# One weight load in each of pairs 13 and 14 is cut by rows: eight transfers of six rows and one of 80

## What is computed

```
logits = (hf @ router_w + router_b)
top_logits, top_idx = lax.top_k(logits, TOP_K)
gates = jax.nn.softmax(top_logits, axis=-1)
...
gu = xb @ w_gate_up[e] + b_gate_up[e]
gate, up = gu[..., :D_FF_EXPERT], gu[..., D_FF_EXPERT:]
gate = jnp.minimum(gate, SWIGLU_LIMIT)
up = jnp.clip(up, -SWIGLU_LIMIT, SWIGLU_LIMIT)
act = (up + 1.0) * gate * jax.nn.sigmoid(SWIGLU_ALPHA * gate)
return act @ w_down[e] + b_down[e]
```

## Time and profile before

| | us |
|---|---|
| median of three runs (1192.39 to 1192.57) | 1192.5 |
| the profiled execution, its own time | 1192.38 |
| its span, first to last instruction | 1190.7 |
| TensorE matmul busy in it | 1105.9 (93%) |
| VectorE busy | 350.4 (29%) |
| ScalarE busy | 167.0 (14%) |
| share of the span in the chain that ended last: TensorE | 65% |
| the same: DMA | 31% |

### The profile page before, as it was taken

How to read it: one execution, slowest core, us unless ns; L and a number is a source line. 1 busy time by engine, 2 the same in 40 slices (tenths; PEclk the granted TensorE clock), 3 DMA queues, 4 the chain that set the end, 5 groups by cost and what they waited for, 6 DMA issues and landing times.

```text
span 1190.7 us, 15332 instructions
## 1 busy us (share of the span) xinstructions
PE 1105.9 (93%) x6539; PEld 539.3 (45%) x6539; DVE 350.4 (29%) x740; ACT 167.0 (14%) x272; POOL 4.0 (0%) x23
## 2 busy tenths in 40 slices
PE   7999999999999999999898799998799898989897
PEld 5889886763434343433332334333334333333332
DVE  4685234463312212212222122212112212121313
ACT  3431234441100000010101000101010101010002
POOL 1000000000000000000000000000000000000000
PEclk9999999999999999999998899999899999999999
DMA  9832414677999999999999999999999999999994
GB/s 336 302 142 72 141 71 116 279 280 302 429 426 429 427 427 431 432 430 428 429 430 429 427 428 431 428 433 425 428 429 432 428 432 427 434 424 435 423 427 170
DMA packets 39053, 436.04 MB, mean 366 GB/s; under 512 B 5813, under 2 KB 5898, under 8 KB 20330
## 3 DMA queue, kind: packets, MB, share of 16 engines
q1 hardware_dynamic: 37066, 433.67, 86.7%
q10 hardware_dynamic: 1920, 1.34, 0.6%
HBM read 433.95 MB, written 1.05 MB: 365 GB/s over the span
## 4 chain that ended last, share of the span: by engine, by line
PE 65%; DMA 31%; issue 2%; DVE 1%; ACT 1%; SPq 0%; DVEq 0%; PEldq 0%
DMA ring<-in_w_down 27%; PE ps L1970 19%; PE ps L2010 16%; PE ps L1548 4%; PE ps L1659 4%; PE ps L2025 3%; PE ps L1605 3%; DMA ring<-in_w_gate_up 3%; PE ps L1940 3%; PE ps L1528 3%; PE ps L1655 2%; PE ps L1716 2%; PE ps L1792 1%; PE ps L1836 1%; DMA ring<-in_w_in 1%
## 5 line engine op out<-in xcount | busy, mean ns | idle before, releaser
L2010 PE MATMUL ps<-ring,work 128*64 128x512 f32 x1024 | 238.2, 613 | 32.0 <-DMA ring<-in_w_down 27.8
L1970 PE MATMUL ps<-work 128*64 128x512 f32 x1024 | 234.4, 600 | 0.2 <-DVE work L1394 0.2
L1970 PE MATMUL ps<-ring,work 128*64 128x512 f32 x1024 | 225.5, 593 | 8.2 <-DMA ring<-in_w_gate_up 8.2
L2010 PEld LDWEIGHTS ps<-ring,work 128*64 128x64 f32 x1024 | 78.5, 140 | 166.6 <-issue 155.0
L1970 PEld LDWEIGHTS ps<-ring,work 128*64 128x64 f32 x1024 | 72.5, 137 | 156.4 <-issue 141.9
L1970 PEld LDWEIGHTS ps<-work 128*64 128x64 f32 x1024 | 73.9, 139 | 138.7 <-issue 132.1
L1427 DVE COPY work<-ps 128x512 f32<-128x512 f32 x16 | 11.1, 691 | 241.6 <-PE ps L1528 241.6
L1404 DVE TENSOR_SCALAR work<-ps 128x512 f32<-128x512 f32 x32 | 22.0, 686 | 196.3 <-PE ps L1528 196.3
L1439 DVE COPY work<-ps 128x512 f32<-128x512 f32 (+1 forms) x16 | 11.1, 691 | 206.4 <-PE ps L2010 206.4
L787 ACT ACTIVATE ps<-work 128x512 f32<-128x512 f32 x32 | 19.3, 602 | 365.1 <-DVE work L1404 365.1
L2025 PE MATMUL ps<-work 128*128 128x512 f32 (+1 forms) x132 | 59.7, 608 | 10.4 <-ACT work L794 10.2
(11 more groups left out here) (237 smaller groups left out, 722.4 us busy)
## 6 DMA issues: line engine op xcount, KB each, us to landing
work<-in_w_gate_up SPq DMA_DIRECT2D x64, 2048.0 KB, 34.6
ring<-in_w_gate_up SPq DMA_DIRECT2D x24, 4096.0 KB, 31.8
ring<-in_w_down SPq DMA_DIRECT2D x22, 4096.0 KB, 35.7
ring<-in_w_down SPq DMA_DIRECT2D x19, 2048.0 KB, 21.7
ring<-in_w_gate_up SPq DMA_DIRECT2D x16, 2048.0 KB, 20.0
ring<-in_w_in SPq DMA_DIRECT2D x7, 2048.0 KB, 15.5
ring<-in_xattn_w_kv SPq DMA_DIRECT2D x2, 2048.0 KB, 13.8
ring<-in_w_out SPq DMA_DIRECT2D x2, 2048.0 KB, 8.2
```

Source lines behind the costliest of these rows:

```text
L1970: last = nc.tensor.matmul(bank(b)[p], xg_T[k][:, kb, :], quad_columns(w[:, kk, D_MODEL * (q // 2):D_MODEL * (q // 2 + 1)], q % 2), start=F ...
L2010: last = nc.tensor.matmul(bank(Y_BANK + y)[p], act_T[k][:, b, HALF * c:HALF * c + HALF], w[:, b, 512 * q:512 * q + 512], start=False, stop ...
```

## The change

`load_chunk` gets a branch for chunk 0 of pairs 13 and 14. There the 128 rows of 16 KB are not issued as one transfer but as nine: eight transfers of six rows (rows 0 to 47), then one of the remaining 80 rows. Each of the nine adds 16 to `slot_loaded6`, and the counts that TensorE and the later loads wait for are raised by 8 per changed load. The bytes, their source and the place are the same, and so are all other loads and their order.

```diff
+BY_SIXES = [(13, 0), (14, 0)]
+SIXES, SIX_ROWS = 8, 48
...
+        def loads_by_sixes(i, s):
+
+            return SIXES * len([1 for j, c in BY_SIXES if j <= i and chunk_place(j, c)[0] == s])
...
-            return uses_before_experts(s) + use
+            return uses_before_experts(s) + use + loads_by_sixes(i, s)
...
-            return uses_before_experts(s) + len([1 for i in range(PAIRS) for c in range(PAIR_CHUNKS)
-                                                 if chunk_place(i, c)[0] == s and first_pass_chunk(i, c)[1] is not None])
+            return uses_before_experts(s) + loads_by_sixes(PAIRS, s) + len(
+                [1 for i in range(PAIRS) for c in range(PAIR_CHUNKS)
+                 if chunk_place(i, c)[0] == s and first_pass_chunk(i, c)[1] is not None])
...
-                sp.dma_start(place(s), src).then_inc(S(f"slot_loaded{s}"), 16)
+                if isinstance(i, int) and (i, c) in BY_SIXES:
+                    for r in range(0, SIX_ROWS, 6):
+                        sp.dma_start(place(s)[r:r + 6], src[r:r + 6]).then_inc(S(f"slot_loaded{s}"), 16)
+                    sp.dma_start(place(s)[SIX_ROWS:], src[SIX_ROWS:]).then_inc(S(f"slot_loaded{s}"), 16)
+                else:
+                    sp.dma_start(place(s), src).then_inc(S(f"slot_loaded{s}"), 16)
```

## The result

The changed kernel took **1229.17 us** (median of 4 runs, 1226.34 to 1233.06) against 1192.53 us (4 runs, 1192.39 to 1193.64): a ratio of 1.0307, 95% interval 1.0276 to 1.0339. It is 36.6 us slower, where 3.1 us less were forecast, and it lies above every rival's time. The profiled execution took 1226.34 us, its span is 1224.6 us, 33.9 us more than before.

A forecast was written before the change was run, and what follows sets the result against it. It took the expert weight loads, ending with their slowest engine, as the bound. All six engines being early ones gave -3.1 us, other terms nothing: 1192.5 - 3.1 = 1189.4 us, range 1188.4 to 1193.0.

The forecast's parts named there:

- The bound: Expert weight loads from 400 to 1150 us: DMA at 429 GB/s sets the end, plus about 39 us of unchanged work.
- Bytes: In the two changed loads: none added; six engines get 10 rows more, +6.1 us, ten get 6 fewer, -3.7 us.
- The late engines: At the end of the loads, eight engines finish at about 1166 to 1167, the other eight between 1173 and 1176.
- rival 1: Late engines are among the six: one ends 3 to 6 us later, 1197.5 us; chance 0.17.
- the instruction queue: Inferred cause of the gap between engines: its 59 packets, 0.97 MB, cost eight engines 7 us each.
- Issue on SP: At 966 and 1024: eight more issues per changed load, 3.4 us at most, hidden by a 15.1 us gap; cost nothing.
- More transfers: On the six engines: 16 more transfers, at most 0.06 us each, 1 us in all; taken as 0.
- The rows behind the price: Four 512 KB pieces near the end, at 414 and 406 GB/s in place of 429, bounding a small transfer's cost.
- The changed load itself: Lands earlier on its late engines, 3.1 us later per load on the six, which lead by some 6 to 10 us.
- TensorE's matmuls and their clock stay: On TensorE: the change leaves matmuls and clock as they were, and the raised counts add no wait.
- rival 3: Small transfers hold their six engines longer than their bytes; at 1 us each, 1205 us; chance 0.03.
- Rival 2: Nothing is moved between engines, each keeps about its share: 1192.5 us, the same within 0.2%; chance 0.10.

The follow-up runs named there:

- even_64: Kernel before the change, chunk 0 of pairs 13 and 14 cut into every second row, then every fourth from 1 and from 3: 1191.11 us, ratio 0.9995.
- columns8: Kernel before the change, chunk 0 of pairs 13 and 14 loaded as eight transfers of all 128 rows and 512 columns each: 1194.03 us, ratio 1.001.
- spread_sixes: Kernel before the change, same two loads cut into 64 and 32 spread rows, five sixes of rows 20 apart and two rows: 1204.77 us, ratio 1.0104.
- rows48_80: Kernel before the change, chunk 0 of pairs 13 and 14 cut into rows 0-47 and rows 48-127: 1214.85 us, ratio 1.0181.
- low_to: SBUF places of low_64 filled from the HBM rows of even_64, against the kernel before the change: 1220.16 us, ratio 1.0245.
- low_64: Kernel before the change, chunk 0 of pairs 13 and 14 cut into rows 0-63, 64-95 and 96-127: 1220.33 us, ratio 1.025.
- even_to: SBUF places of even_64 filled from the HBM rows of low_64, against the kernel before the change: 1191.27 us, ratio 0.9987.

## Why the prediction was wrong

**The bound: right.** The transfers decide. Time lost on them came out in full: 27.3 us by the rate and 6.6 by one late engine make the 33.9 us of the span, with the same 39.4 us behind the last wait. `even_64` and `columns8`, at 429 and 424 GB/s from 960 to 1165, took the time of before within 1 us.

**Bytes: the step that failed.** It priced a row at 0.61 us of its engine's time, whichever partitions the row goes to, and got +6.1 us for six engines and -3.7 us for ten. The runs put in its place that a transfer also needs its rows spread over the 16 groups. A six of neighbours has four rows in one group, and eight such sixes and the 80 rows count 40 in place of 8. This step cost 27.3 us of rate in two loads, where the prediction had none. The 19.5 us per load of the strict sum lie near the measured 18.3 by luck: they are too much for crowding alone, and the 18.3 hold the late engine too. What the prediction did not ask is which part of the on-chip memory each row enters.

**The late engines.** The gap of the earlier trace rows is there, and the prediction's arithmetic for it held, but on the side of rival 1. The forecast wanted all six among the early engines, -3.1 us. The ends of the loads show one late engine among them: alone for about 10 us where the rows give an estimate of 9.8, and 6.6 us of the time. So, as far as the ends show it, the kernel would have become some 6 us slower even without the loss by the rate. What makes eight engines late, the instruction queue by the prediction, was not tested. `spread_sixes`, a gentler move of rows between the same engines, has the late engine too, still crowds some groups and cost 11.7 us. A transfer that spreads evenly over 16 groups has at least 16 rows, one for every engine, so it moves nothing between engines; that leaves no way by evenly spread cuts to take a row off a late engine. This last is argued from the runs, not tried in every form.

**Issue on SP: right.** 2.7 us for eight, hidden; the next issue came 12.1 and 17.6 us later. (In the earlier trace rows the gaps after the issue are 15.4 and 15.1 us, not 15.1 both times.)

**More transfers: right as far as tested.** Taken as nothing; `columns8`, with 14 more transfers, gave 0.8 us at a ratio of 1.001. Six-row transfers have no such test. The rows behind the price were read too wide: the four pieces are issued from 1141.92 on the earlier trace rows and take 30.0 to 32.4 us to land, so in 1162 to 1164 only the early engines can have been at them.

**The changed load itself: wrong.** "It is not late for anybody" did not hold: one of the six was late itself, the stream as a whole ran at half rate while the load passed, and the chain waited 48 to 49 us at a time on the loads around it, where it had waited 35 to 42. And "TensorE's matmuls and their clock stay" did not hold: the waits took the clock to 0.56 in one stretch and the mean matmul of the down projection from 613 to 623 ns. Of TensorE's 10.2 us more of busy time the chain shows little: one piece of 32 matmuls has 8.44 us, where the others have 7.1.

**The rivals.** The sign to look for under rival 3, a rate clearly under 429 near 1000 and 1060, is what the trace shows. Its mechanism is not: small transfers are free when they are columns. The Trainium skill's fixed cost of about 2 us per DMA (DMA: Bandwidth & Descriptors, section "Anatomy of one DMA"), from which an estimate of 1221 us stood there, comes near 1229 by accident: if 2 us held the engine for each transfer, `columns8` would have cost some 30 us as well, an estimate from the page's figure, and it cost 0.8. Rival 1 asked for a tail past 1179 and 3 to 6 us: the tail is there, one engine alone until about 1210, and its part is 6.6 us. It is a part only, as `rows48_80`, with equal rows for every engine, lost 21.7 us without it. Rival 2 is excluded by the size. None of the cases held the 27.3 us lost by the rate, so the range, 1188.4 to 1193.0 us, was a range of my cases and not of the unknown: the one cost not bounded by any row was that of a partial set of partitions in a full stream, since the trace of before has no such load.

## What to carry to other kernels

Where loads run back to back, cut a 128-row load by columns, or by rows with a stride that keeps each part even over all 128 (every second, every fourth); a cut into blocks of neighbouring rows, or into sets that reach fewer than 16 groups, costs 6 to 21 us per 2 MB here. Count, per transfer, the rows in the fullest group before running it; a count of 8 was free here, and more than 8 never was. Look at the end of the loads for an engine that goes on alone: cuts of six rows left one behind by 10 us and more. And read GB/s next to the DMA share: the share stayed at 1 while the rate was half.

## What the runs showed of the hardware

- Transfers that together crowd some groups of partitions slow the whole stream from 429 GB/s to 182 to 246 (counts of 16 and more) for 10 to 30 us per 2 MB load, and the DMA share does not show it. The Trainium skill's rule on the 16 ports (SBUF — State Buffer, section "Door 1: The DMA port swizzle") names the same groups and agrees in direction. Its sentence in the section "Can I just issue two DMAs to hit both halves?", that only one transfer over all 128 partitions reaches all 16 ports, is too narrow if it is read as all 128 rows: transfers of every second or every fourth row reached all 16 groups and were free too.
- The loss is longer than the load. 48 and 80 rows make 4.9 us more by the count and 10.8 us in time, 7.7 us where the engines are still close together.
- Transfers of six rows leave one engine behind. With two such loads its share of 0.06 goes on alone for 10 to 13 us, where the cuts with equal rows have 3 us at most.
- The source does not matter: 64 rows of HBM in one piece or every second row made 0.2 us of difference (`low_to` and `low_64`, `even_to` and `even_64`).
- A transfer of 256 KB by columns is as good as its share of one of 2 MB: 16 of them in a full queue, ratio 1.001.
